# A decoder step's first stages: tokens turned raw, the inverse norm multiplied into each projection tile

## The reference, cut to what matters

```
def rmsnorm(x, g):
    y = xf * lax.rsqrt(jnp.mean(xf * xf, axis=-1, keepdims=True) + NORM_EPS)
    return (y * g.astype(F32)).astype(x.dtype)

h = rmsnorm(x, lp['ln_mix_g'])
proj = h @ lp['w_in']          # 2048 -> 4352 columns
# columns of an RWKV group: mixed with the token before, ps = p + (shifted - p) * mu
# columns of an attention group: used as they are
```

## Time and profile before

| | us |
|---|---|
| median of 3 runs (lowest, highest) | 1930.25 (1927.11, 1934.85) |
| the profiled execution's own time | 1926.11 |
| its span, first to last instruction | 1924.4 |
| PE busy in the span | 1795.4 |
| block 2 begins (first ACT instruction) | 34.12 |
| first matmul of the next block | 311.42 |

### The profile page before, as it was taken

The page is one execution under the profiler, slowest core; times in us unless marked ns, Lnnn a source line. Parts: engine busy times, 40 slices in busy tenths (PEclk is TensorE's granted clock), DMA queues, the critical chain, the costliest instruction groups (busy, mean ns, idle before and its releaser), DMA issues. The chain is left out here.

```text
span 1924.4 us, 35948 instructions
## 1 busy us (share of the span) xinstructions
PE 1795.4 (93%) x15607; PEld 1232.4 (64%) x15607; DVE 687.8 (36%) x1296; ACT 481.6 (25%) x836; POOL 111.7 (6%) x115
## 2 busy tenths in 40 slices
PE   5999998997989999998999999999999999999995
PEld 5999987875667799786455554554554544555442
DVE  4437776545568443753411111111111111111113
ACT  4446654441223322732311011011110000000001
POOL 0000002300101000000000000000000000000000
PEclk8999999998999999999999999999999999999998
DMA  7644550224535772547899999999999999999997
GB/s 225 162 127 127 136 132 11 69 36 126 167 117 221 235 191 67 184 136 303 309 385 428 421 424 427 424 421 418 422 421 427 421 425 420 419 426 423 422 426 267
DMA packets 191391, 545.99 MB, mean 284 GB/s; under 512 B 39227, under 2 KB 146844, under 8 KB 163566
## 3 DMA queue, kind: packets, MB, share of 16 engines
q1 hardware_dynamic: 184080, 518.03, 70.4%
q0 software_dynamic: 6768, 26.09, 4.4%
q10 hardware_dynamic: 438, 0.32, 0.1%
HBM read 524.86 MB, written 28.06 MB: 287 GB/s over the span
## 5 line engine op out<-in xcount | busy, mean ns | idle before, releaser
L2976 PE MATMUL p_u<-w_expert,xgT 128*64 128x256 f32 x2048 | 239.2, 387 | 26.7 <-DMA w_expert<-in_w_up_dram 26.6
L2976 PE MATMUL p_g<-w_expert,xgT 128*64 128x256 f32 x2048 | 232.1, 379 | 1.7 <-DVE xgT L3079 0.9
L2976 PEld LDWEIGHTS p_u<-w_expert,xgT 128*64 128x64 f32 x2048 | 148.9, 140 | 108.7 <-DMA w_expert<-in_w_up_dram 33.7
L2992 PE MATMUL p_y<-w_expert,hidT 128*64 128x512 f32 x960 | 217.5, 595 | 0.5 <-DVE hidT L3091 0.5
L2976 PEld LDWEIGHTS p_g<-w_expert,xgT 128*64 128x64 f32 x2048 | 146.7, 137 | 89.1 <-issue 18.4
L2944 PE MATMUL p_xg<-low,slot_sel 128*64 128x512 f32 x768 | 177.1, 596 | 0.0
L2992 PEld LDWEIGHTS p_y<-w_expert,hidT 128*64 128x64 f32 x960 | 66.3, 137 | 125.4 <-issue 124.7
L3084 DVE CAST row<-rowf 128x1 int32<-128x1 f32 x32 | 4.9, 154 | 356.9 <-POOLq L3225 356.9
L3171 ACT ACTIVATE act_g<-p_g 128x256 f32<-128x256 f32 x32 | 12.3, 383 | 442.0 <-PE p_u L2976 442.0
L2944 PEld LDWEIGHTS p_xg<-low,slot_sel 128*64 128x64 f32 x768 | 52.3, 137 | 79.4 <-issue 73.6
L426 PE MATMUL in_acc<-x_high,w_in_high 128*128 128x320 f32 (+2 forms) x560 | 93.2, 319 | 8.2 <-ACT w_in_high L457 8.2
(11 more groups left out here) (601 smaller groups left out, 2439.1 us busy)
## 6 DMA issues: line engine op xcount, KB each, us to landing
w_expert<-in_w_gate_dram SPq DMA_DIRECT2D x64, 2048.0 KB, 21.6
w_expert<-in_w_up_dram SPq DMA_DIRECT2D x64, 2048.0 KB, 23.2
w_expert<-in_w_down_dram SPq DMA_DIRECT2D x60, 2048.0 KB, 19.8
w_in_raw<-in_w_in_dram SPq DMA_DIRECT2D x32, 1024.0 KB, 5.8
ho_raw<-in_w_out_dram SPq DMA_DIRECT2D x12, 1024.0 KB, 6.5
q_lat<-in_w_out_dram SPq DMA_DIRECT2D x4, 1024.0 KB, 8.1
mem_k_s<-in_cache_mem_k_dram SPq DMA_DIRECT2D x8, 512.0 KB, 7.5
mem_v_s<-in_cache_mem_v_dram SPq DMA_DIRECT2D x8, 512.0 KB, 11.5
```

The costliest lines, as they stand in the source:

```text
L2976: mm = pe.matmul(acc[SL * h:SL * h + SL, 0:FF // 2], xgT[:, t, g // 2, :], w[g][:, FF * t + FF // 2 * h:FF * t + FF // 2 * h + FF // 2], s ...
L2992: mm = pe.matmul(p_y[SL * h:SL * h + SL, 512 * b:512 * b + 512], hidT[:, j, g, :], tile, start=(g == 0 and j == 0), stop=(g == 1 and j == 1))
```

## The change

In block 1 each token tile is turned once, raw. The turned tile stays in its PSUM bank (seven banks in a ring) while DVE multiplies it with the gain into `hT` and ACT copies it to `S.xT`. The gain vector comes by a DMA of its own and is turned first. Rounding and subtracting go by quarters of a tile. The norm is no longer taken in this block; the rounding of the first weight tile's high part is moved into it, and SP's wait for the tables is moved to the start of block 2.

In block 2 ACT squares `S.xT` (four pieces of 1280 elements a partition), DVE adds the 16 slices in four halvings, PE sums over the partitions with a matrix of ones behind tile 0, ACT takes the root, DVE the reciprocal, `inv`. Each accumulator is multiplied by `inv` on DVE: in place for an RWKV tile (and ACT waits for that, `scaled`), and straight into the destination for an attention tile, where before ACT and DVE took turns with a copy.

The diff, cut to its core:

```diff
 (load_front, PE)
+                pe.wait_ge(gain_in, 16)
+                pe.transpose(p_gain, gain_rows[:, :], S.ident[0:DT, 0:DT]).then_inc(gain_turned, 1)
                 turn_raw(0)
...
-                turn_raw(1)
-                turn_scaled(0)
-                turn_raw(2)
-                turn_scaled(1)
-                turn_scaled(2)
+                turn_raw(1)
+                turn_raw(2)
 (load_front, ACT: square and root removed)
+                for u in range(12):
+                    copy(u)
+                    high(u)
+                act.wait_ge(S.raw_in[0], 16)
+                act.copy(S.wh0[:, :, 0:IN_TILES[0][2]], S.raw[0][:, :, 0:IN_TILES[0][2]]).then_inc(first_high, 1)
 (load_front, DVE)
+                for u in range(12):
+                    gains(u)
+                    if u >= 2:
+                        low(u - 2)
+                low(10)
+                low(11)
...
 (project_in, SP)
+                sp.wait_ge(S.tables_in, 16)
 (project_in, PE)
+                    if s == 0:
+                        pe.wait_ge(S.tables_in, 16)
+                        pe.wait_ge(added, 4)
+                        pe.matmul(p_last[:, 0:T], S.table("ones"), total, start=True, stop=True).then_inc(x_summed, 1)
 (project_in, ACT)
-                split(0)
+                split(1)
+                for n in range(4):
+                    act.activation(squares[:, 4 * T * n:4 * T * n + 4 * T], S.xT[:, 4 * n:4 * n + 4, :].rearrange("p t n -> p (t n)"), ACT.Square).then_inc(squared, 1)
+                split(2)
+                act.wait_ge(x_summed, 1)
+                act.activation(mean_root, p_last[:, 0:T], ACT.Sqrt, bias=S.eps[:, :], scale=1.0 / D).then_inc(x_rooted, 1)
...
-                    act.wait_ge(done, s + 1)
                     if t < 28:
+                        act.wait_ge(scaled, MIXED.index(s) + 1)
 (project_in, DVE)
                 split(0)
+                for n in range(4):
+                    half = 8 * T >> n
+                    dve.wait_ge(squared, 4)
+                    if n:
+                        dve.wait_ge(added, n)
+                    dve.tensor_tensor(squares[:, 0:half], squares[:, 0:half], squares[:, half:2 * half], ALU.add).then_inc(added, 1)
+                    if n == 0:
+                        split(1)
+                dve.wait_ge(x_rooted, 1)
+                dve.reciprocal(inv, mean_root).then_inc(x_inverted, 1)
...
+                    dve.wait_ge(done, s + 1)
                     if t < 28:
+                        dve.tensor_tensor(bank[0:m, 0:T], bank[0:m, 0:T], inv[0:m, :], ALU.mult).then_inc(scaled, 1)
...
+                    else:
+                        dve.tensor_tensor(dst[t], bank[0:m, 0:T], inv[0:m, :], ALU.mult).then_inc(other, 1)
```

More of the change, by code:

```diff
@@ L149, in load_front @@
         rows = sb("vector_rows", [128, 2, 128]); x = sb("x_tokens", [128, 3, D]); prev = sb("prev_rows", [8, RPROJ])
[L150 to L155, removed]
+        gain_rows = sb("gain_rows", [DT, 128]); gain = sb("gain_columns", [128, DT])
+        RING = 7
+        p_r = [ps(f"p_r{i}") for i in range(RING)]; p_v = ps("p_v"); p_prev, p_gain, p_rows = p_v[:, 0:224], p_v[:, 224:224 + DT], p_v[:, 256:512]
+        cleared = sem("cleared"); rows_in = sem("vec_in"); gain_in = sem("gain_in"); x_in = [sem(f"x_in{i}") for i in range(3)]; prev_in = sem("prev_in"); ident_in = sem("ident_in")
+        gain_turned = sem("gain_turned"); gain_kept = sem("gain_kept"); vec_turned = sem("vec_turned"); vec_done = sem("vec_done"); prev_turned = sem("prev_turned"); prev_done = sem("prev_done")
+        raw_turned = sem("raw_turned"); raw_copied = sem("raw_copied"); gained = sem("x_gained"); high_made = sem("x_high_made"); low_made = sem("x_low_made"); first_high = sem("first_w_high")
         names = dict(w0='rwkv_w0', a0='rwkv_a0', k_k='rwkv_k_k', k_a='rwkv_k_a', gn_g='rwkv_gn_g', gn_b='rwkv_gn_b', ln_mix='ln_mix_g', q_norm='mla_q_norm_g',
@@ L158, in load_front, with place, bank @@
         cols = [(128 * t, 128) for t in range(24)] + [(3072, 96), (3168, 96), (3264, 128), (3392, 128)]
-        at = [128 * i for i in range(3)]
         hT, xT = S.mix, S.xT
-        squares = [S.xh[:, :, :].rearrange("p t n -> p (t n)")[:, D * e:D * e + D] for e in (0, 1, 0)]
+        groups = [(i, q) for i in range(3) for q in range(4)]
+        def place(u):
+            i, q = groups[u]
+            return slice(4 * q, 4 * q + 4), slice(128 * i, 128 * i + TILE[i])
+        def bank(u):
+            n = TILE[groups[u][0]]
+            return p_r[u % RING][:, 0:4 * n].rearrange("p (t n) -> p t n", t=4)
         with nc.Block() as block:
@@ L243, in copies @@
[L243 to L263, removed]
+                def copy(u):
+                    act.wait_ge(gained, u + 1)
+                    t, at = place(u)
+                    act.copy(xT[:, t, at], bank(u)).then_inc(raw_copied, 1)
+                def high(u):
+                    t, at = place(u)
+                    act.copy(S.xh[:, t, at], hT[:, t, at]).then_inc(high_made, 1)
@@ L275, in gain @@
[L275 to L283, removed]
-                    dve.wait_ge(high_made, i + 1)
-                    dve.tensor_tensor(S.xl[:, :, at[i]:at[i] + n], hT[:, :, at[i]:at[i] + n], S.xh[:, :, at[i]:at[i] + n], ALU.subtract).then_inc(low_made, 1)
@@ L344, in project_in @@
         k_k, k_a, r_k = S.vec('k_k'), S.vec('k_a'), S.vec('r_k')
+        inv = S.table("spare")[:, 0:T]; squares = S.mix[:, :, :].rearrange("p t n -> p (t n)"); total = squares[:, 0:T]; mean_root = squares[:, T:2 * T]
+        squared = sem("x_squared"); added = sem("x_added"); x_summed = sem("x_summed"); x_rooted = sem("x_rooted"); x_inverted = sem("x_inverted"); scaled = sem("scaled")
         acc = [ps(f"in_acc{i}") for i in range(4)]; p_z = [ps("p_z0"), ps("p_z1")]; p_last = ps("p_last")
```

97 lines of the change are left out of this document (35 added, 62 removed).

## The result

The changed kernel takes 1950.33 us, median of 5 runs (1946.45 to 1952.77), the kernel before 1930.25 on the same chip (1927.11 to 1934.85): 1.0103 times, 95% interval 1.0089 to 1.0117. It is 20 us slower; 8 were forecast, and the range ended at 1945. On another chip it was 1.0092 (1.0072 to 1.0112) times. The profiled execution took 1952.77, its span is 1951.0. Two single executions of the experiments further down, of 3506.51 us (kernel before) and 5596.1 us (with 83 transposes), stand far outside all others and are left out of the ratios.

The account below looks back on a forecast made before the run. PE, busy 93% of the span, was taken as the bound. 4.3 us gained up to tile 2 less 12.5 lost at the tiles made 8.2 us slower, forecast 1938 us median; range 1933 to 1944, 1925 to 1945 with the hidden case.

Parts of the forecast that it names:

- block 1 and the seam: Projection starts at 24.1 instead of 35.65, 11.5 us gained; after the halvings' wait tile 2 starts at 46.8, 4.3 left.
- The table load: Before the root in block 2: 1.28 us by the trace, against 2.66 with the skill's drain; hidden either way but for 0.1.
- the mechanism at the tiles: Tiles 13 to 34: multiplying after DVE's next subtraction delays ACT's reading and rounding, so PE waits; 12.5 us lost.
- Tile 29: Projection tile 29: PE waits 3.5 us for ACT's rounding in place of 1.07.
- PE's delay is swallowed: Projection tiles: slow clock after waits costs nothing there, because ACT and DVE, not PE, are the late ones.
- The clock rival: New tile waits lower PE's clock, up to 1.33 us each, 14.9 lost in all, 1945; chance 0.12 with later block 2.
- the later block 2: Block 2 begins later than forecast, making the kernel slower; shares the chance of 0.12 with the clock rival.
- The term: The tiles' loss from tile 2 to the heads' block: 12.5 us.
- the seam: Tiles 0 to 2: PE waits 5.1 us for DVE's halvings, then runs slower; 4.3 of 11.5 us gained are left.
- All later stages start later by this, since nothing there has a date of its own.: Everything behind the projection shifts by the same 8.2 us, next block at about 319.6 in place of 311.42.
- the multiplication was not hidden: Rival, projection tiles: the multiplication is hidden, late reading costs only 1.0 us, 3.3 gained, 1927; chance 0.15.
- the front's gain did not survive: Rival, seam: halvings end before tile 0, so the 11.5 us are kept but for 1, 1920; chance 0.07.

Follow-up runs that it names:

- with 83 transposes: The kernel before with 83 tiny 8x8 transposes on PE ahead of its first projection matmul; 1.0041 times the kernel before.
- the product first: The changed kernel with DVE multiplying tile s before subtracting for tile s+1, same instructions in another order; 1.0054 times the kernel before.
- the combined kernel without transposes: The changed kernel with DVE's multiplication ahead of its subtraction and the matmul of ones behind tile 1, no transposes added; 1.0041 times the kernel before.

## Why the prediction was wrong

**Right: block 1 and the seam.** PE's start was met to 0.1 us, tile 2 to 0.9. The table load came out by the trace's rule: 1.28, and the root 0.01 behind it (42.49 + 1.28 = 43.77, 43.78), so the drain that the Trainium skill gives in "ScalarE: Activation LUTs", What ACT_TABLE_LOAD costs, does not show.

**Right: the mechanism at the tiles.** The waits sum to 12.6 us where 14.2 were forecast. DVE subtracted for tile 18 until 173.67, ACT had rounded for tile 19 at 180.39: 6.7 us, forecast 6.6 (the terms of the forecast, 0.48 + 0.47 + 1.5 + 1.28 + 1.1 + 1.9, make 6.7). That most of it is the place was shown by the order alone: 9.8 of 15.4 us. Tile 29 was mis-sized: a wait of 2.28 us, forecast 3.5.

**Mis-sized: "PE's delay is swallowed".** The clock rival, with the later block 2, was given 0.12, with the reason that rows show a fall only after light work of PE, and these waits follow full tiles. It fell all the same: three groups behind waits of 3.47, 3.94 and 2.28 us took 1.4, 1.5 and 1.1 us more. The Trainium skill's rule on pauses in "TensorE: Matmul & The Clock Gate", HAM oscillation — how this bites in real kernels, that work behind a pause starts cold, is borne out at these three tiles, and not behind the waits of 2.08 and 0.83 us. From tile 2 to the heads' block 13.8 us were lost (from -3.4 to +10.4), 12.5 forecast. The term was 1.3 us short, the seam 0.9, together the 2.2 between 8.2 and 10.4. That it came so near is in part luck: the slow groups, held to be nothing, took 4.0 us, the waits were 1.6 under their forecast, and two waits for low weights that the kernel before has (0.80 each) were gone, swallowed as the prediction said. The length of a wait alone does not decide: after 1.88 us the group took 2.61 with the product first, and 4.15 in the combined kernel without transposes.

**The step that failed: "All later stages start later by this, since nothing there has a date of its own."** PE's stream has. The block behind was held to be a fixed length, and it grew by 12.0 us: some 7 by the 45 matmuls missing ahead of it, up to 4.7 by the clock. The numbers for it lay ready: the count of PE instructions of both kernels, and the stops "issue" in the block of small matmuls, 128 apart in the trace of the kernel before. Neither was read, since nothing there was changed. They would have given the new places of the stops, not their price. With 7 us for the place the sum is 8.2 + 7 = 15, and 1945 for the median; 2.2 more from the term above and a part of the clock's 4.7 make the 20.

The rivals: the multiplication was not hidden, and the front's gain did not survive. The clock rival named 1945 and had the sign of the miss, but not the place where most was lost.

## What to carry to other kernels

Where an engine goes through hundreds of small instructions in a few us, its stream's refills show as idle time "issue" at a fixed distance, and an edit anywhere ahead of it moves them: count the instructions of that engine added and removed before such a stretch, waits and branches too, and shift the place by dummies in an idle time before a difference is put down to the edit. An added step on one engine costs by its place in the order: give first what another engine waits for. And a time saved ahead of a wait for data or for a busier engine is worth only what that one leaves.

## What the runs showed of the hardware that was not expected

- PE stops at every 128th matmul (with its weight load) of its stream when it gets there too fast: 1.4 to 2.5 us for each of the first two stops of the heads' block, at 12 to 18 ns a matmul. These two end 3.5 to 4.0 us apart (325.62 and 329.64; 315.80 and 319.25). In all instructions of PE the grid is 256: all 70 stops of over 0.3 us in 13 traces stand on it, to within one instruction, and an edit of 45 matmuls some 280 us ahead moved them.
- Tiny transposes of 8 x 8 on PE are not free in bulk: 83 took 2.22 us, 128 took 3.34, some 26 ns each, while 128 of the heads' small matmuls took 1.49 us, 12 ns each.
- The same stretch of some 432 matmuls without a wait took 17.49 us at a granted clock of 1.00, 19.15 at 0.91 and 23.86 at 0.71, in unchanged code.
